# A two-block transformer kernel: latent attention's transposed weights in three rotating PSUM banks and copied by two engines, value products spread over units, one row store moved to a later stage

## The chip, the cores and the metric

The program runs on one core of one Trainium2 chip. Its engines work side by side: TensorE (PE; its weight loads are listed apart as PEld), VectorE (DVE), ScalarE (ACT), GpSimd (POOL), and SyncE (SP), whose queue issues most of the DMAs. The metric is the device time of one execution in microseconds (us), as a median of runs.

## The reference

Two blocks run one after the other on 512 tokens of width 1024. The part that matters here is the beginning of the first block:

```python
sc, scc = silu(c), silu(c_ctx)
shift1, scale1, gate1, ... = split(sc @ w_mod + b_mod)     # only the first two are needed at once
h  = modulate(rms_norm(x, norm1_g), shift1, scale1)        # 512 tokens
hc = modulate(rms_norm(ctx, norm1_g), ...)                 # 256 context tokens
proj = h @ w_in                                            # keys, values, gates, queries, ...
# gated linear attention (GLA): log decays, cumulative sums in chunks of 64 tokens, exponentials of them,
# states per chunk, outputs
# latent attention: 8 query heads, 2 key heads, 512 queries, 512 + 256 keys, head width 128
sc_ = einsum('bkgqd,bknd->bkgqn', q, k) * 128 ** -0.5
p   = softmax(sc_, axis=-1)
y_att = einsum('bkgqn,bknd->bkgqd', p, v)
```

Hyena filters, the merge of three branches, a mixture of 16 experts and the second block follow.

## The kernel before, in words

The program is a row of stages. Each is a block in which every engine has its own list of instructions, written out by hand; semaphores order the engines inside, and at the end of a block all engines meet at a barrier before any of them begins the next. Weights go through a ring of four SBUF slots of 1 MB (`Ring`): SP issues a chunk as soon as the chunk four places ahead of it has been released. A chunk of `w_in` is split by ScalarE into a rounded high part (line 124) and by GpSimd into the low remainder (line 130), and TensorE multiplies high by high, high by low and low by high (lines 240, 243, 244).

The stages that the change and the prediction touch, in order:

- `mod_stage` (0 to 45 us): silu(c) and its products with `w_mod`. SP issues the eight chunks of `w_mod`, then the store of silu(c) from SBUF to the DRAM row `silu_row` (line 350; 128 partitions x 8 single numbers, written element by element), then four loads for the router (line 353), then the first four chunks of `w_in`, and waits until the store and the router loads have landed (`inputs_in`, line 355). `silu_row` is read again only in the merge stage at 685 us (line 456).
- `gla_project_stage` (45 to 175 us) runs `groups_stage` with `gla_decay_work` beside it: functions hung into each engine's list at places (group, place). ScalarE's last ones were the copies of the transposed key tiles for units 2 and 3 (`copy(act, 2)`, line 1162) and the exponential of the chunk totals `K.tot` (line 1169), both behind the four silu evictions of the last group (line 1032).
- `gla_chunk_stage` (175 to 221 us): the chunk states (TensorE lines 1358 and 1367, VectorE's recurrences at line 1456).
- `qk_stage` (221 to 317 us): queries and keys. GpSimd loads `k_cos`, `k_sin` and `k_swap` first; TensorE needs `k_swap` at line 735.
- `latent_attention_stage` (317 to 453 us), written in `attention_stage`: 8 heads of 4 blocks of 128 queries, 32 units in all. It is the only stage that calls this function.

A unit `a` of the attention goes through these steps: TensorE's scores (line 1520, 512 + 256 columns in two PSUM banks, alternating between banks 0-1 and 2-3), VectorE's maximum (line 1563) and bias (1569), ScalarE's exponential with its row sum (1546), VectorE's reciprocal (1574) and scaling (1576), TensorE's six 128 x 128 transposes (1528) into PSUM banks 4 and 5, VectorE's copy of all 768 columns to SBUF `PT` (1584). The loops are skewed: in round `a` TensorE does the scores of unit a and the transposes of unit a - 2. After the last unit of a head it does the head's six value products of 512 columns in one piece (called at line 1536, recorded as line 263), and ScalarE copies the result out (1553). The waits that order this for TensorE:

```python
pe.wait_ge(exp_done, a - 1)      # scores a reuse the banks of unit a-2
pe.wait_ge(normed, b + 1)        # b = a - 2, the block to be transposed
pe.wait_ge(copied, b)            # banks 4, 5 emptied by VectorE's copy of unit b-1
```

A product of fp32 operands is recorded as two MATMUL rows, a transpose as one.

## Time and profile before

| | |
|---|---|
| median of 3 runs | 2266.17 us (2265.34 to 2267.31) |
| the profiled execution's own time | 2269.96 us |
| its span (first to last instruction) | 2268.2 us |
| TensorE busy, share of the span | 2080.7 us, 92% |
| VectorE, ScalarE, GpSimd | 1173.8 (52%), 853.9 (38%), 577.8 us (25%) |
| mean granted TensorE clock | 0.963 |
| stage of latent attention | 317.5 to 452.8 us |

A busy TensorE is not the same as a TensorE at its peak: a matmul's record begins when it is issued and its end is modelled, so records overlap. What a group of them costs is read from start to start.

### The profile page before, as it was taken

What the parts mean: (1) busy time and instruction counts of PE and PEld (TensorE: products, weight loads), DVE (VectorE), ACT (ScalarE), POOL (GpSimd) and SP (SyncE); (2) the same over time, 40 slices, a digit from 0 to 9 for tenths busy, and PEclk for the clock granted to TensorE, in tenths of its full rate; (3) what the DMA queues carried; (4) which work ended last, traced back from release to release, by engine and by line L of the source; (5) the groups of instructions that cost most, each with busy time, mean ns of one, the idle gap of its engine ahead of it and who ended that gap; (6) DMA issues with size and microseconds to landing.
All of it is one profiled execution on the core that took longest, in us unless ns stands there. A gap on an engine that the chain in (4) does not pass through costs nothing. (4 is left out here: it accounts for less than half of the span.)

```text
span 2268.2 us, 23240 instructions
## 1 busy us (share of the span) xinstructions
PE 2080.7 (92%) x9310; PEld 1584.0 (70%) x9310; DVE 1173.8 (52%) x1391; ACT 853.9 (38%) x1059; POOL 577.8 (25%) x191
## 2 busy tenths in 40 slices
PE   5998998899879999889999989999799998999997
PEld 2666754474348888577777767687688876878886
DVE  2444556545884576468888667305703246223223
ACT  3532223234222223357777547514422323212221
POOL 0322200130014344120000023440144444433441
PEclk8999999999989999989999999999999999999999
DMA  7224210031015555279999942231022332322310
GB/s 246 93 74 163 75 37 1 0 112 33 0 37 195 167 195 181 89 285 367 381 382 385 334 163 93 79 106 34 21 92 88 100 119 94 110 93 74 100 48 38
DMA packets 172014, 299.67 MB, mean 132 GB/s; under 512 B 10211, under 2 KB 67754, under 8 KB 171912
## 3 DMA queue, kind: packets, MB, share of 16 engines
q1 hardware_dynamic: 166600, 279.93, 35.8%
q0 software_dynamic: 3008, 9.93, 1.2%
q10 hardware_dynamic: 2304, 8.39, 0.9%
q8 instruction: 71, 1.16, 0.2%
q14 instruction: 31, 0.25, 0.0%
HBM read 275.09 MB, written 23.13 MB: 131 GB/s over the span
## 5 line engine op out<-in xcount | busy, mean ns | idle before, releaser
L130 POOL TENSOR_TENSOR region<-weights,region 128x2048 fp32r<-128x2048 f32 (+2 forms) x94 | 370.8, 3946 | 986.4 <-ACT region L124 736.4
L240 PE MATMUL ps<-region 128*128 128x512 f32 (+1 forms) x1336 | 529.0, 396 | 43.7 <-DVE region L576 12.8
L243 PE MATMUL ps<-region 128*128 128x512 f32 (+1 forms) x1336 | 519.2, 389 | 0.0
L244 PE MATMUL ps<-region 128*128 128x512 f32 (+1 forms) x1336 | 519.2, 389 | 0.0
L240 PEld LDWEIGHTS ps<-region 128*128 128x128 f32 x1336 | 258.8, 194 | 106.9 <-DVE region L130 20.8
L243 PEld LDWEIGHTS ps<-region 128*128 128x128 f32 x1336 | 258.6, 194 | 51.7 <-issue 3.6
L244 PEld LDWEIGHTS ps<-region 128*128 128x128 f32 x1336 | 258.4, 193 | 50.2
L124 ACT ACTIVATE region<-weights 128x2048 fp32r<-128x2048 f32 (+2 forms) x98 | 158.7, 1622 | 291.2 <-PE ps L244 244.6
L2982 DVE TENSOR_TENSOR region<-weights,region 128x2048 fp32r<-128x2048 f32 x92 | 209.4, 2288 | 47.0 <-ACT region L2891 46.8
L2891 ACT ACTIVATE region<-weights 128x2048 fp32r<-128x2048 f32 x92 | 176.2, 1918 | 68.2 <-DMA weights<-moe_w_up 29.8
L281 PE MATMUL ps<-region 128*128 128x512 f32 x480 | 190.0, 396 | 7.2 <-DVE region L4085 4.5
L3928 POOL TENSOR_TENSOR region<-weights,region 128x2048 fp32r<-128x2048 f32 x30 | 143.0, 4781 | 203.8 <-ACT region L4038 178.3
L283 PE MATMUL ps<-region 128*128 128x512 f32 x480 | 187.0, 390 | 0.0
L282 PE MATMUL ps<-region 128*128 128x512 f32 x480 | 186.8, 389 | 0.0
L2780 PE MATMUL ps<-region 128*128 128x512 f32 x384 | 154.2, 401 | 12.6 <-issue 8.0
L2781 PE MATMUL ps<-region 128*128 128x512 f32 x384 | 151.2, 394 | 0.0
L2782 PE MATMUL ps<-region 128*128 128x512 f32 x384 | 151.2, 394 | 0.0
L2404 DVE TENSOR_TENSOR region<-ps,region 128x512 f32<-128x512 f32 x48 | 33.1, 690 | 198.1 <-PE ps L244 198.1
L281 PEld LDWEIGHTS ps<-region 128*128 128x128 f32 x480 | 90.2, 188 | 29.2 <-DVE region L4089 6.0
L4093 DVE TENSOR_TENSOR region<-ps,region 128x512 f32<-128x512 f32 x64 | 44.3, 692 | 124.2 <-PE ps L283 124.2
L4038 ACT ACTIVATE region<-weights 128x2048 fp32r<-128x2048 f32 x32 | 60.3, 1910 | 122.1 <-PE ps L4015 118.2
L283 PEld LDWEIGHTS ps<-region 128*128 128x128 f32 x480 | 90.1, 188 | 19.0
(442 smaller groups left out, 2740.5 us busy)
## 6 DMA issues: line engine op xcount, KB each, us to landing
weights<-w_in SPq DMA_DIRECT2D x54, 1024.0 KB, 5.3
weights<-moe_w_gate SPq DMA_DIRECT2D x32, 1024.0 KB, 7.8
weights<-moe_w_up SPq DMA_DIRECT2D x32, 1024.0 KB, 8.8
weights<-moe_w_down SPq DMA_DIRECT2D x32, 1024.0 KB, 7.7
region<-w_mod_rows SPq DMA_DIRECT2D x32, 512.0 KB, 4.6
weights<-w_mlp_in SPq DMA_DIRECT2D x16, 1024.0 KB, 5.2
weights<-w_mlp_out SPq DMA_DIRECT2D x16, 1024.0 KB, 5.0
weights<-w_mod SPq DMA_DIRECT2D x8, 1024.0 KB, 9.4
```

Of the source, the lines that this page charges most:

```text
L124: act.activation(flat(self.part(K, n, 0)), flat(r.view(n)), ACT.Copy).then_inc(self.hi_done, 1)
L130: eng.tensor_tensor(flat(self.part(K, n, 1)), flat(self.ring.view(n)), flat(self.part(K, n, 0)).bitcast(F32), ALU.subtract).then_inc(self. ...
L240: ins = pe.matmul(out, l_hi, r_hi, start=(start and k == 0), stop=False)
L243: pe.matmul(out, l_hi, r_lo, start=False, stop=False)
L244: ins = pe.matmul(out, l_lo, r_hi, start=False, stop=(stop and k == kt - 1))
L281: pe.matmul(out, w_hi, x_hi, start=(n == 0), stop=False)
L282: pe.matmul(out, w_hi, x_lo, start=False, stop=False)
L283: last = pe.matmul(out, w_lo, x_hi, start=False, stop=(n == len(triples) - 1))
L2780: pe.matmul(K.ps[:, bank, :], x_hi[:, x, :], w_hi[:, k, :], start=(start and k == 0), stop=False)
L2781: pe.matmul(K.ps[:, bank, :], x_hi[:, x, :], w_lo[:, k, :], start=False, stop=False)
L2891: act.activation(flat(part(c, 0)), r.slots[n % RING][:, :], ACT.Copy).then_inc(hi_done, 1)
L2982: dve.tensor_tensor(flat(part(c, 1)), r.slots[n % RING][:, :], flat(part(c, 0)).bitcast(F32), ALU.subtract).then_inc(r.used, 1)
```

## The change

There are three edits.

1. Latent attention. The transposes of a unit go as four (128 x 512) into one bank and two (128 x 256) into another, out of banks 4, 5 and 7 in rotation. VectorE copies the four, ScalarE the two. TensorE waits for ScalarE's copy of unit b - 2 ahead of the first four, and for VectorE's copy of unit b - 1 ahead of the other two. The six value products of head h are put behind the transposes of the next four units, 1, 2, 1 and 2 of them.
2. The store of silu(c) is taken out of `mod_stage` and issued as SP's first DMA in `qk_stage`, which waits for it at its end.
3. In `gla_decay_work` the exponential of the totals moves to ScalarE's place (3, 1), right behind the other exponentials, and the copies for units 2 and 3 to place (4, 0), ahead of the last group's evictions.

```diff
@@ -346,13 +346,10 @@
             sp.dma_start(K.xT, T["xT"].rearrange("(t p) n -> p t n", p=P)).then_inc(x_in, 16)
             sp.dma_start(K.hcT, T["ctxT"].rearrange("(t p) n -> p t n", p=P)).then_inc(ctx_in, 16)
             r.issue_until(sp, n0 + 2 * GROUPS)
-            sp.wait_ge(act_ready, 1)
-            sp.dma_start(K.silu_row.rearrange("o (t p) -> p (o t)", p=P), sc[:, :, 0],
-                         allow_slow_non_contiguous=True).then_inc(inputs_in, 16)
             for dst, src in router_loads(K):
                 sp.dma_start(dst, src).then_inc(inputs_in, 16)
             r.issue_until(sp, n0 + 2 * GROUPS + RING)
-            sp.wait_ge(inputs_in, 80)
+            sp.wait_ge(inputs_in, 64)
 
         @block.scalar
         def _(act):
@@ -628,7 +625,7 @@
     r, T = K.ring, K.T
     split = K.split1
     (raw_done, sq_done, ss_done, mean_done, rec_done, rstd_done, gained, swap_done, t1_done, t2_done, added, out_done,
-     v_done, v_copied, ctx_done, zero_done, select_done, rows_done, cols_done, scale_rec, *out_signals) = K.signals(28 + 1)
+     v_done, v_copied, ctx_done, zero_done, select_done, rows_done, cols_done, scale_rec, row_out, *out_signals) = K.signals(29 + 1)
     gla, last = GlaOutput(K, out_signals), ST - 1
     sq, t, t1, t2, rec = K.at(100, 2, S), K.at(104, 3, S), K.at(110, 2, S), K.at(114, 2, S), K.at(118, 2, S)
     cos, sin, swap = K.at(124, S), K.at(126, S), K.at(128, P)
@@ -671,7 +668,10 @@
         @block.sync
         def _(sp):
             K.start(sp)
+            sp.dma_start(K.silu_row.rearrange("o (t p) -> p (o t)", p=P), K.sc[:, :, 0],
+                         allow_slow_non_contiguous=True).then_inc(row_out, 16)
             r.issue_until(sp, n0 + 6 + RING)
+            sp.wait_ge(row_out, 16)
 
         @block.tensor
         def _(pe):
@@ -1162,11 +1162,13 @@
             act.activation(K.kend[:, :, u, :], z_of(u).rearrange("p (t c) -> p t c", c=P), ACT.Copy)\
                 .then_inc(copied, 1)
 
+    def exps_and_totals(act):
+        exps(act, 2)
+        act.activation(K.tot[:, :, :], K.tot[:, :, :], ACT.Exp, scale=1 / 16).then_inc(copied, 1)
+
     def last(act):
-        copy(act, 2)
         for c in chains:
             act.wait_ge(c, 2 * STEPS)
-        act.activation(K.tot[:, :, :], K.tot[:, :, :], ACT.Exp, scale=1 / 16).then_inc(copied, 1)
         act.wait_ge(copied, 5)
 
     def step(dve, u, j, f):
@@ -1228,7 +1230,7 @@
     return {"loads": 3, "pool": pool,
             "pe": {(1, 0): lambda pe: decays(pe, 0), (3, 0): turn_and_decays, (4, 0): lambda pe: turn(pe, 2)},
             "act": {(1, 0): lambda act: logs(act, 0), (2, 0): lambda act: exps(act, 0), (3, 0): copy_and_logs,
-                    (3, 1): lambda act: exps(act, 2), (4, 2): last},
+                    (3, 1): exps_and_totals, (4, 0): lambda act: copy(act, 2), (4, 2): last},
             "dve": {(1, 0): both(sums, 0), (2, 1): both(scale, 0), (3, 0): both(sums, 2), (3, 2): both(scale, 2)}}
 
 
@@ -1487,7 +1489,7 @@
 
 
 
-    s_done, max_done, bias_done, exp_done, rec_done, normed, turned, copied, o_done, o_copied = K.signals(10)
+    s_done, max_done, bias_done, exp_done, rec_done, normed, turned, copied, rest_copied, o_done, o_copied = K.signals(11)
     NB, NJ = heads * ST, nk // P
     Pb = K.at(tmp, 3, nk)
     PT = K.at(tmp + 3 * nk / 256, 2, NJ, S)
@@ -1507,12 +1509,23 @@
         def sbank(a):
             return K.ps[:, 2 * (a % 2):2 * (a % 2) + 2, :].rearrange("p b n -> p (b n)")[:, 0:nk]
 
-        def tbank():
-            return K.ps[:, 4:6, :].rearrange("p b n -> p (b n)")[:, 0:nk].rearrange("p (j q) -> p j q", q=P)
+        def turned_at(b):
+
+            low, high = ((4, 5, 7)[(2 * b + i) % 3] for i in range(2))
+            return (K.ps[:, low, :].rearrange("p (j q) -> p j q", q=P),
+                    K.ps[:, high, 0:nk - 512].rearrange("p (j q) -> p j q", q=P))
+
+        def value_steps(a):
+
+            h, part = divmod(a - 2 - ST, ST)
+            if not 0 <= h < heads:
+                return h, ()
+            cuts = [i * NJ // ST for i in range(ST + 1)]
+            return h, range(cuts[part], cuts[part + 1])
 
         @block.tensor
         def _(pe):
-            for a in range(NB + 3):
+            for a in range(NB + 2 + ST):
                 if a < NB:
                     if a >= 2:
                         pe.wait_ge(exp_done, a - 1)
@@ -1522,33 +1535,48 @@
                 b = a - 2
                 if 0 <= b < NB:
                     pe.wait_ge(normed, b + 1)
+                    low, high = turned_at(b)
+                    if b >= 2:
+                        pe.wait_ge(rest_copied, b - 1)
+                    for j in range(4):
+                        ins = pe.transpose(low[:, j, :], Pb[:, b % 3, j * P:(j + 1) * P], K.ident[:, :])
+                    ins.then_inc(turned, 1)
                     if b >= 1:
                         pe.wait_ge(copied, b)
-                    for j in range(NJ):
-                        ins = pe.transpose(tbank()[:, j, :], Pb[:, b % 3, j * P:(j + 1) * P], K.ident[:, :])
+                    for j in range(4, NJ):
+                        ins = pe.transpose(high[:, j - 4, :], Pb[:, b % 3, j * P:(j + 1) * P], K.ident[:, :])
                     ins.then_inc(turned, 1)
-                b = a - 3
-                if b >= 0 and b % ST == ST - 1:
-                    h = b // ST
-                    pe.wait_ge(copied, b + 1)
-                    if h >= 1:
-                        pe.wait_ge(o_copied, h)
-                    accumulate(pe, K.ps[:, 6, :], [(values(h, j), PT[:, h % 2, j, :]) for j in range(NJ)])\
-                        .then_inc(o_done, 1)
+                h, part = value_steps(a)
+                for j in part:
+                    if j == 0:
+                        pe.wait_ge(copied, ST * (h + 1))
+                        pe.wait_ge(rest_copied, ST * (h + 1))
+                        if h >= 1:
+                            pe.wait_ge(o_copied, h)
+                    ins = pe.matmul(K.ps[:, 6, :], values(h, j), PT[:, h % 2, j, :], start=(j == 0), stop=(j == NJ - 1))
+                    if j == NJ - 1:
+                        ins.then_inc(o_done, 1)
 
         @block.scalar
         def _(act):
-            for a in range(NB + 3):
+            for a in range(NB + 2 + ST):
                 if a < NB:
                     act.wait_ge(bias_done, a + 1)
                     if a >= 3:
-                        act.wait_ge(turned, a - 2)
+                        act.wait_ge(turned, 2 * (a - 2))
                     act.activation(Pb[:, a % 3, :], sbank(a), ACT.Exp, bias=st[:, 1, a:a + 1],
                                    scale=scale if scales is None else scales[:, a:a + 1],
                                    accum_out=st[:, 2, a:a + 1]).then_inc(exp_done, 1)
-                b = a - 3
-                if b >= 0 and b % ST == ST - 1:
+                b = a - 2
+                if 0 <= b < NB:
                     h = b // ST
+                    dest_of = PT[:, h % 2, :, (b % ST) * P:(b % ST + 1) * P]
+                    act.wait_ge(turned, 2 * b + 2)
+                    if h >= 2:
+                        act.wait_ge(o_done, h - 1)
+                    act.activation(dest_of[:, 4:NJ, :], turned_at(b)[1], ACT.Copy).then_inc(rest_copied, 1)
+                h, part = value_steps(a)
+                if NJ - 1 in part:
                     act.wait_ge(o_done, h + 1)
                     act.activation(dest(h), K.ps[:, 6, :], ACT.Copy).then_inc(o_copied, 1)
                 if first and a in (NB - 3, NB - 1):
@@ -1577,11 +1605,12 @@
                         .then_inc(normed, 1)
                 b = a - 2
                 if b >= 0:
-                    dve.wait_ge(turned, b + 1)
                     h = b // ST
+                    dest_of = PT[:, h % 2, :, (b % ST) * P:(b % ST + 1) * P]
+                    dve.wait_ge(turned, 2 * b + 1)
                     if h >= 2:
                         dve.wait_ge(o_done, h - 1)
-                    dve.tensor_copy(PT[:, h % 2, :, (b % ST) * P:(b % ST + 1) * P], tbank()).then_inc(copied, 1)
+                    dve.tensor_copy(dest_of[:, 0:4, :], turned_at(b)[0]).then_inc(copied, 1)
 
 
 def latent_attention_stage(K):
```

On TensorE, in the attention stage, the head boundary stood like this before (line 1520: scores, 1528: transposes, 263: value products):

```order
L1528 MATMUL ps<-ident,region 128x128 x6
L263 MATMUL ps<-region 128x512 x6
L1520 MATMUL ps<-region 128x512
L1520 MATMUL ps<-region 128x256
L1528 MATMUL ps<-ident,region 128x128 x6
L1520 MATMUL ps<-region 128x512
L1520 MATMUL ps<-region 128x256
L1528 MATMUL ps<-ident,region 128x128 x6
```

The same stage now (1533: scores, 1542 and 1547: the four and the two transposes, 1556: value products):

```order
L1533 MATMUL ps<-region 128x512
L1533 MATMUL ps<-region 128x256
L1542 MATMUL ps<-ident,region 128x128 x4
L1547 MATMUL ps<-ident,region 128x128 x2
L1556 MATMUL ps<-region 128x512
L1533 MATMUL ps<-region 128x512
L1533 MATMUL ps<-region 128x256
L1542 MATMUL ps<-ident,region 128x128 x4
L1547 MATMUL ps<-ident,region 128x128 x2
L1556 MATMUL ps<-region 128x512 x2
```

The value products have moved from one piece of six to one or two behind each unit's transposes; their number is the same.

On ScalarE, the end of `gla_project_stage` was (1139: exponentials, 124: high part of a chunk, 1032: evictions with silu, 1162: key copies, 1169: totals):

```order
L1139 ACTIVATE region<-region 128x512 x2
L1139 ACTIVATE region<-region 128x768
L124 ACTIVATE region<-weights 128x2048
L1032 ACT_TABLE_LOAD
L1032 ACTIVATE region<-ps 128x512 x4
L1162 ACTIVATE region<-ps 128x6x128 x2
L1169 ACT_TABLE_LOAD
L1169 ACTIVATE chunk_decay<-chunk_decay 128x36
```

and is now (1167: totals; the copies keep line 1162):

```order
L1139 ACTIVATE region<-region 128x512 x2
L1139 ACTIVATE region<-region 128x768
L1167 ACTIVATE chunk_decay<-chunk_decay 128x36
L124 ACTIVATE region<-weights 128x2048
L1162 ACTIVATE region<-ps 128x6x128 x2
L1032 ACT_TABLE_LOAD
L1032 ACTIVATE region<-ps 128x512 x4
```

The evictions are the last thing that ScalarE does in this stage, and one table load is gone.

On SP, in `mod_stage`, the queue behind the last chunks of `w_mod` was

```order
L350 DMA silu_row<-silu_c 128x8x1
L353 DMA router<-router_w 128x8x16
L353 DMA router<-router_b 128x16
L353 DMA router<-k_upto 128x128
L353 DMA router<-k_slot_no 128x128
L87 DMA weights<-w_in 128x4x128 x2
```

and is now

```order
L350 DMA router<-router_w 128x8x16
L350 DMA router<-router_b 128x16
L350 DMA router<-k_upto 128x128
L350 DMA router<-k_slot_no 128x128
L87 DMA weights<-w_in 128x4x128 x2
```

Everything behind the store moves up by one place.

## Rows read from the trace of the kernel before

**Rows 1.** Timeline, one head of latent attention: start us, duration, engine, line, operation.

```profile
351.87 5.32 PE L263 MATMUL ps<-region 128*128 128x512 f32 x12
...
357.02 1.45 PE L1520 MATMUL ps<-region 128*128 128x512 f32 x4
...
358.31 0.82 PE L1528 MATMUL ps<-ident,region 128*128 128x128 f32 x6
358.51 0.96 DVE L1563 TENSOR_REDUCE region<-ps 128x1 f32<-128x768 f32 x1 [4.82 <-PE ps L1520]
...
358.96 1.46 PE L1520 MATMUL ps<-region 128*128 128x512 f32 x4
...
360.30 0.95 DVE L1584 COPY region<-ps 128x768 f32<-128x768 f32 x1
...
361.40 0.84 PE L1528 MATMUL ps<-ident,region 128*128 128x128 f32 x6 [0.98 <-DVE region L1584]
...
362.95 0.95 DVE L1584 COPY region<-ps 128x768 f32<-128x768 f32 x1
```

**Rows 2.** Groups by line and form: busy us, mean ns of one, idle before.

```profile
L1546 ACT ACTIVATE region<-ps,region 128x768 f32<-128x768 f32 x32 | 31.7, 990 | 51.2 <-DVE region L1569 51.2
L1033 DVE COPY region<-ps 128x512 f32<-128x512 f32 x10 | 6.9, 690 | 63.5 <-PE ps L244 60.9 <-PE ps L263 2.5
L781 ACT ACTIVATE region<-ps 128x256 f32<-128x256 f32 x6 | 2.2, 371 | 3.2 <-PE ps L244 3.2
```

**Rows 3.** Timeline, the last two groups of value products of the stage.

```profile
429.46 5.32 PE L263 MATMUL ps<-region 128*128 128x512 f32 x12
...
443.63 8.50 PE L263 MATMUL ps<-region 128*128 128x512 f32 x12 [1.05 <-DVE region L1584]
```

**Rows 4.** Stretches: length, busy (x) of PE, PEld, DVE, ACT, POOL, clock, DMA share, GB/s.

```profile
357.00:400.00 43.00, 36.97 (x149) 21.02 (x148) 31.02 (x60) 14.76 (x27) 0.00 (x0) 1.00 0.00 1
...
440.00:442.00 2.00, 0.93 (x5) 0.96 (x6) 0.93 (x1) 0.17 (x1) 1.75 (x1) 0.50 0.00 0
```

**Rows 5.** Timeline of SP and VectorE, end of the mod stage and start of the next.

```profile
27.15 0.51 SPq L350 DMA_DIRECT2D silu_row<-silu_c  x1
...
38.20 0.16 DVE L429 SCALAR_TENSOR_TENSOR gains<-mods,vec_cols 128x8 f32<-128x8 f32 x1
38.21 0.43 SPq L353 DMA_DIRECT2D router<-k_slot_no  x1
...
45.18 1.41 DVE L567 SCALAR_TENSOR_TENSOR region<-region,gains 128x512 f32<-128x512 f32 x2 [6.83 <-remote]
```

**Rows 6.** Line 350: us from issue to landing of the store of silu(c).

```profile
DMA to landing us min/median/max: 13.9/13.9/13.9
```

**Rows 7.** A stretch ahead of the store's landing, columns as in rows 4.

```profile
34.00:41.00 7.00, 3.79 (x33) 2.26 (x32) 2.25 (x5) 0.70 (x2) 0.00 (x0) 0.95 0.01 1
```

**Rows 8.** Timeline, end of the GLA projection stage and start of the chunk stage.

```profile
171.00 0.60 ACT L1032 ACTIVATE region<-ps 128x512 f32<-128x512 f32 x1 [2.12 <-PE ps L244]
...
173.02 1.28 ACT L1169 ACT_TABLE_LOAD   x1
174.31 0.23 ACT L1169 ACTIVATE chunk_decay<-chunk_decay 128x36 f32<-128x36 f32 x1
...
175.02 1.12 PE L1358 MATMUL ps<-region 128*64 128x128 f32 x8 [4.06 <-PEq L948]
...
178.09 0.29 DVE L1452 COPY region<-ps 128x128 f32<-128x128 f32 x1 [1.92 <-PE ps L1367]
```

**Rows 9.** A stretch of the chunk stage, columns as in rows 4.

```profile
176.00:178.00 2.00, 2.00 (x32) 1.60 (x30) 0.18 (x1) 0.97 (x1) 1.72 (x3) 0.50 0.54 160
```

**Rows 10.** The qk stage: GpSimd's last load, its us to landing, and its first reader.

```profile
222.64 0.54 POOL L663 DMA_DIRECT2D region<-k_swap  x1
...
229.41 1.02 PE L735 MATMUL ps<-region 128*128 128x512 f32 x2
...
region<-k_swap POOLq DMA_DIRECT2D x1, 64.0 KB, 2.9
```

## The prediction

> **What bounds the kernel now.** I read the stretches first, then one head on the timeline, then the two stage ends that the other edits touch. TensorE is busy for 92% of the span, so time can only come from places where it stands or runs slowly. In latent attention it stands: in 43 us of steady heads it has 36.97 us of records at full clock, VectorE 31.02, ScalarE 14.76 [rows 4]. One head [rows 1]: the value products start at 351.87, the next scores at 357.02, so six products take 5.15 us, 0.86 each. The scores run to 358.31 (1.29 us), the transposes to 358.96 (0.65 us). The bound alternates. While the value products run VectorE waits (4.82 us ahead of the maximum at 358.51); in the other units TensorE waits (0.98 us ahead of the transposes at 361.40) for line 1584, the copy that empties banks 4 and 5. VectorE's pace there is 2.65 us a unit (copy at 360.30 to copy at 362.95). The period of a head, from value products at 351.87 to those at 429.46 five heads later [rows 1, 3], is 77.59 / 5 = 15.52 us. TensorE's own work in it is 5.15 + 4 x 1.29 + 4 x 0.65 = 12.91 us.
>
> At the end of the mod stage all engines wait for DMAs: VectorE's last instruction starts at 38.20, its next at 45.18 [rows 5], behind the store and the router loads. At the end of the GLA projection ScalarE alone works, from 171.6 to 174.54, and TensorE stands for 4.06 us [rows 8].
>
> **Edit 1, latent attention.** The same products and transposes are issued, and as many scores. VectorE's copy shrinks from 768 to 512 columns: 690 ns [rows 2] against 950 ns, 0.26 less, so its pace becomes 2.65 - 0.26 = 2.39 us a unit. ScalarE, busy for 14.76 of 43 us or 1.33 a unit [rows 4], gets a copy of 256 columns, 0.37 us [rows 2]: 1.70. TensorE with spread products has 1.29 + 0.65 = 1.94 plus 0.86 or 1.72, so 2.80 or 3.66 us, on average 3.23. It is the longest of the three in every unit, if nothing it waits for is late. I walked one short unit, starting at TensorE's scores of a. The maximum of a starts 1.49 after them (357.02 to 358.51 in rows 1); the bias is ready some 1.06 later, at 2.55; maximum, bias, reciprocal and scaling of a - 1 take 1.79 (358.51 to 360.30), and the shorter copy what is left of the pace, 2.39 - 1.79 = 0.60: VectorE is through at 3.9. TensorE begins the next round at 2.80, has finished its scores at 4.09, and only then needs the scaled block of a - 1, ready at about 3.4, and 0.43 later, at 4.5, the emptied bank, ready at 3.9. ScalarE's exponential of a (0.99 [rows 2], a hand-over ahead and the reading of its sum behind) ends at about 3.9; TensorE needs it for the scores of a + 2, at 6.46. ScalarE's own copy is then done by 4.3 and needed more than a unit later. So no wait is left in a head, and the closest margin is 0.6 us.
>
> Sum of this edit:
> - Six full heads, 15.52 to 12.91: 6 x 2.61 = 15.7.
> - The lead-in, where no value products are interleaved yet and VectorE sets the pace: four copies of 0.26: 1.0.
> - From the start of head 6's products (429.46) to those of head 7 (443.63) there are 14.17 us [rows 3], with only 5.15 + 1.29 + 3 x 0.65 = 8.4 us of work for TensorE. With the products spread, VectorE's chain runs beneath them; what remains is head 7's wait until ScalarE has copied head 6's result out (one bank for the output), 0.25 + 0.60 = about 0.9. Saved: 14.17 - 9.3 = 4.9.
> - The last head's products took 8.50 instead of 5.32 us [rows 1, 3], because TensorE's clock stood at its lower level, 0.50, in a stretch in which it had work for only 0.93 of 2 us [rows 4]. With the chain beneath the products that stretch is gone, so I take the 3.2 us.
>
> Together 24.8. The bounds of this term: no gain beyond TensorE's own work is possible, so 25 is the most. At the other end, each unit could lose the hand-over of a buffer at each of the two waits of its transposes; one hand-over is 0.15 us (the copy of 360.30 ends at 361.25, TensorE starts at 361.40 in rows 1), so 28 x 0.30 = 8.4, and 16 at least.
>
> **Edit 2, the store.** It was issued at 27.15 and landed 13.9 us later, at 41.05 [rows 5, 6]. From 34 to 41 all DMA engines together move 1 GB/s and are busy for 1% [rows 7]. The queue is silent for 7 us with the store at its head; the router loads land only after it and SP can issue the last of them only at 38.21. Without the store the router loads should land by about 36 and the first chunks of `w_in` soon after. Then VectorE's own chain, ending at 38.36, ends the stage. A barrier takes 0.48 (ScalarE's last end at 174.54, TensorE's start at 175.02 [rows 8]), so the next stage starts at 38.84 and not at 45.18: 6.3 earlier. Bounds: the stage can't end before its own arithmetic, so 6.3 is the most; if the 1024 short reads of `router_w` are what is slow, hardly anything is won, 0.5.
>
> In the qk stage the store is SP's first DMA. The next chunk has to wait for TensorE to free a slot, so none stands behind the store. GpSimd's three loads go out at the same time. `k_swap` lands at 222.64 + 2.9 = 225.5 and is first read at 229.41 [rows 10], a cover of 3.9 us. If the store's 7 us delayed it fully, TensorE would wait 3.1. I take 0 and keep 3.1 for the range.
>
> **Edit 3, the GLA end.** Gone from behind the last eviction are two key copies, a table load and an exponential; the end moves from 174.54 to 171.60, 2.9 us [rows 8]. The copies now stand ahead of the evictions, where TensorE's next bank comes every 2.7 us and ScalarE waits 2.12 of it [rows 8]: the copies, 1.4 us between 171.60 and 173.02, hide there. Then a second effect. TensorE's pause falls from 4.06 to about 1.2 us. The chunk stage ran its first products at half clock (0.50 at 176 to 178 [rows 9]), and VectorE, whose chain of recurrences sets that stage's first part, could start only at 178.09, 3.1 us after TensorE. With the clock kept, about half of that, 1.4 us, is saved. Bounds: 0 if the clock falls anyway, 1.6 at most.
>
> The Trainium skill (ScalarE: Activation LUTs, "What ACT_TABLE_LOAD costs") puts a switch of tables at 2.66 us, a drain of 1.38 us included. In this trace the activation starts 1.29 us after the load does [rows 8], so the drain doesn't show; by the page edit 3 would be worth 1.4 us more. I go by the row.
>
> **Sum.** 24.8 + 6.3 + 2.9 + 1.4 = 35.4 us. The profiled execution took 2269.96 us (span 2268.2), 3.8 above the median of the runs; there the sum gives 2234.6. Against the median of 2266.17 it is 2230.8, **2231**. All else only shifts: at both ends of latent attention the DMA queues move nothing [rows 4], so the later stages find the same state.
>
> **The rivals.**
> - The heads don't become bound by TensorE alone: gaps of up to 0.3 us in each unit remain at the two-part transposes. For it speaks the margin of 0.6 us only, against it that scores and transposes already follow each other without a gap after two satisfied waits [rows 1]. Edit 1 is then worth 16: 2239.
> - `router_w` is the slow transfer, not the store. For it: also 1024 descriptors. Against it: the store, ahead in the queue, itself landed only at 41.05 [rows 5, 6]. Edit 2 is worth 0.5: 2237.
> - The store holds up GpSimd's three loads in the qk stage: plus 3.1, 2234. The Trainium skill (DMA: Bandwidth & Descriptors, on issuing engines) has all queues share the same 16 DMA engines, which is this case; no row here shows two queues with a store of this kind.
> - Slower: the rotation makes a unit serial. TensorE's transposes wait for a copy by ScalarE, which stands behind an exponential, which waits for VectorE, which waits for TensorE. The chain of one unit is 3.9 to the end of its exponential as walked above, and about 0.8 for reciprocal and scaling, 0.65 for transposes and 0.9 for a copy and its hand-over: 6.2 us. With two units in flight it costs 3.1 a unit, under 3.23. If only one were in flight, 32 x 6.2 = 198 us against 135, that is 63 us more in edit 1, less the 10.6 of the others: 2319. It decides from 4.2 us a unit (15.52 / 4 = 3.88, plus those 10.6 us over 32 units). The waits as written, on units b - 1 and b - 2, allow two; little speaks for it.
>
> **How the numbers follow.** Forecast as summed 0.62, gaps 0.13, `router_w` 0.11, qk stage 0.10, slower 0.02, the rest for something unseen. 2231 belongs to the first; its own spread is 2227 to 2235. The range has to take in the second and third, so up to 2241; below, the edges of the terms give 2227, and a little of the 3.8 us by which two executions of one kernel differ makes it 2226. A change below 0.2% (4.5 us) could not be told from none here. Faster 0.97, same 0.015, slower 0.015.
>
> **What would show it.** In the changed kernel's trace: TensorE without idle time from the first head to the last, period 12.9 us; VectorE waiting 0.4 to 1.3 us in every unit instead of 4.8 once a head; clock 1.00 to the stage's end, the last products 5.3 us; the next stage after the mod stage at 38.8; the last activation of the GLA projection a silu eviction, and VectorE's first copy in the chunk stage 1.6 us after TensorE's start; `k_swap` read without a wait. The prediction is wrong if VectorE or ScalarE shows up as what releases the transposes in the heads, or if the DMA silence at 34 us stays.

## The result, and the profile after

The changed kernel takes 2252.09 us (median of 4 runs, 2248.19 to 2254.9) beside 2266.74 for the kernel before: ratio 0.9934, 95% interval 0.9916 to 0.9951. That is 14.7 us faster where 35 were forecast, and 11 us above the upper end of the range. A second comparison of the same two kernels gave 0.9895 (0.9874 to 0.9915), 24 us. The two intervals meet end to end (0.9915 and 0.9916) without overlapping, so comparisons scatter by more than one interval tells; both lie short of the forecast's 0.984. A few us are therefore read from the lengths of stages below, and not from whole times.

The first instruction of TensorE (in the GLA projection of VectorE) after each barrier cuts the profiled executions into stages. Lengths in us:

| stage | before | after | difference | forecast |
|---|---|---|---|---|
| mod stage | 45.18 | 39.76 | -5.42 | -6.3 |
| GLA projection | 129.84 | 124.53 | -5.31 | -2.9 |
| chunk stage | 46.12 | 44.82 | -1.30 | -1.4 |
| qk stage | 96.39 | 102.65 | +6.26 | 0 |
| latent attention | 135.70 | 116.62 | -19.08 | -24.8 |
| all that follows | 1814.97 | 1818.02 | +3.05 | 0 |
| span | 2268.2 | 2246.4 | -21.8 | -35.4 |

Three rows are missed by more than 2.5 us: qk, attention and what follows. (The profiled executions lie 21.8 us apart and the medians 14.7: the profile before took longer than any of its four runs, the profile after is that of its fastest.) I take what the forecast had right first. Timeline of latent attention, as rows 1:

```profile
339.58 1.45 PE L1533 MATMUL ps<-region 128*128 128x512 f32 x4
...
340.87 0.60 PE L1542 MATMUL ps<-ident,region 128*128 128x128 f32 x4
341.07 0.96 DVE L1591 TENSOR_REDUCE region<-ps 128x1 f32<-128x768 f32 x1 [1.19 <-PE ps L1533]
...
341.31 0.38 PE L1547 MATMUL ps<-ident,region 128*128 128x128 f32 x2
...
341.53 1.02 PE L1556 MATMUL ps<-region 128*128 128x512 f32 x2
...
343.88 0.96 DVE L1591 TENSOR_REDUCE region<-ps 128x1 f32<-128x768 f32 x1 [0.32 <-PE ps L1533]
...
344.33 1.88 PE L1556 MATMUL ps<-region 128*128 128x512 f32 x4
...
352.52 1.45 PE L1533 MATMUL ps<-region 128*128 128x512 f32 x4
```

No wait stands on TensorE in this head. It takes 352.52 - 339.58 = 12.94 us (forecast 12.91), and VectorE waits 0.32 or 1.19 a unit (forecast 0.4 to 1.3). The two ends of the stages, as rows 5 and 8:

```profile
39.06 0.16 DVE L426 SCALAR_TENSOR_TENSOR gains<-mods,vec_cols 128x8 f32<-128x8 f32 x1
39.76 0.75 DVE L564 SCALAR_TENSOR_TENSOR region<-region,gains 128x512 f32<-128x512 f32 x1 [0.54 <-DVE gains L426]
```

```profile
163.39 0.60 ACT L1032 ACTIVATE region<-ps 128x512 f32<-128x512 f32 x1 [2.12 <-PE ps L244]
...
164.29 0.66 PE L1360 MATMUL ps<-region 128*64 128x128 f32 x8 [0.94 <-PEq L948]
...
166.02 0.29 DVE L1454 COPY region<-ps 128x128 f32<-128x128 f32 x1 [0.57 <-PE ps L1369]
```

The mod stage ends by VectorE's arithmetic, with a wait of 0.54 us where 6.83 stood, and from 34 to 41 us the DMA queues move 253 GB/s where they moved 1 [rows 7]. A silu eviction is ScalarE's last instruction in the GLA projection, TensorE pauses for 0.94 us instead of 4.06 [rows 8], and VectorE's first copy comes 1.73 us behind TensorE (forecast 1.6).

Now the losses. The qk stage, timeline of SP, GpSimd and TensorE, as rows 10:

```profile
209.21 0.40 SPq L671 DMA_DIRECT2D silu_row<-silu_c  x1
...
210.61 0.54 POOL L660 DMA_DIRECT2D region<-k_swap  x1
...
222.13 1.35 PE L735 MATMUL ps<-region 128*128 128x512 f32 x2 [4.58 <-DMA region<-k_swap]
```

and the DMAs of 190 to 300 us (KB of one, median us from issue to landing):

```profile
DMA packets 4406, 6.97 MB, mean 63 GB/s; under 512 B 1184, under 2 KB 1184, under 8 KB 4400
...
region<-k_cos POOLq DMA_DIRECT2D x1, 256.0 KB, 11.7
...
region<-k_swap POOLq DMA_DIRECT2D x1, 64.0 KB, 11.4
silu_row<-silu_c SPq DMA_DIRECT2D x1, 4.0 KB, 9.3
```

`k_swap` took 11.4 us instead of 2.9 [rows 10], behind a store of 4 KB. TensorE waited 4.58 us for it, and its clock then was 0.64 from 222 to 225 us. Together the stage lost 6.3.

In latent attention one place is off, in the first unit after the last head's scores have begun to run out:

```profile
407.01 4.50 POOL L130 TENSOR_TENSOR region<-weights,region 128x2048 fp32r<-128x2048 f32 x1 [124.05 <-ACT region L124]
407.03 4.90 DVE L1604 TENSOR_SCALAR region<-region 128x768 f32<-128x768 f32 x1
...
411.99 1.11 PE L1542 MATMUL ps<-ident,region 128*128 128x128 f32 x4 [3.45 <-DVE region L1604]
...
413.32 3.62 PE L1556 MATMUL ps<-region 128*128 128x512 f32 x4
...
416.85 4.53 POOL L130 TENSOR_TENSOR region<-weights,region 128x2048 fp32r<-128x2048 f32 x1 [5.34 <-ACT region L124]
...
417.70 0.69 DVE L1613 COPY region<-ps 128x512 f32<-128x512 f32 x1 [2.06 <-PE ps L1542]
```

VectorE's scaling, 0.62 us everywhere else, took 4.90. GpSimd's subtraction (the low part of the next stage's first weight chunk) had begun 0.02 us earlier, and the scaling ended 0.42 after it. TensorE stood for 3.45 us and did its next products at half clock (from 413 to 416 us the granted clock is 0.50: 1.2 GHz and not 2.4). The row at 417.70 narrows it: VectorE's copy out of PSUM ran at its usual 0.69 us beneath the second subtraction. What the subtraction stops is the scaling, which reads and writes SBUF; in all seven profiled executions with edit 1 and the subtraction in this place, this one and those below, one scaling takes 4.90 or 4.91. The Trainium skill says this (SBUF — State Buffer, "Who interferes with whom"): VectorE and GpSimd share a pair of SBUF ports, whoever issues first holds it for the whole instruction, the other blocks, and a scalar multiplication can be of the kind that needs it. This trace agrees, with 4.90 against 0.62 us. In the kernel before, the same two instructions met in the other order:

```profile
429.80 0.62 DVE L1576 TENSOR_SCALAR region<-region 128x768 f32<-128x768 f32 x1
430.04 4.76 POOL L130 TENSOR_TENSOR region<-weights,region 128x2048 fp32r<-128x2048 f32 x1 [141.31 <-ACT region L124]
```

There the scaling came first and kept its 0.62 us, and it was the subtraction that took longer, 4.76 instead of 4.50 us.

### The profile page after: what moved, and what is told of

The parts are those of the page before. It is cut to its first block and busy times, and to the rows that moved or that the text cites. A ratio compares the mean times of both kernels' runs of the same rounds, so it can differ in the third digit from the quotient of the medians.

```text
span 2246.4 us, 23296 instructions
## 1 busy us (share of the span) xinstructions
PE 2074.2 (92%) x9310; PEld 1584.6 (71%) x9310; DVE 1172.9 (52%) x1391; ACT 861.1 (38%) x1090; POOL 578.7 (26%) x191
```

## The experiments

The theory after these readings: the three edits do what the forecast said, and two collisions, one that it had missed and one that it had put at nothing, take back 6 us each (store against `k_swap`, subtraction against scaling). The rival: the rest is lost downstream, because later stages meet the DMA queues in another state.

**The changed kernel again, and each edit alone** (the hunks of the diff above for attention, for the store, or for `gla_decay_work`, on the kernel before).

> The changed kernel once more, for its ratio and for a second profile. Theory 1 (the missing gain was lost in two places ahead of 430 us: TensorE's wait for k_swap with its clock behind it, about 6 us, and a 3.45 us stall of TensorE at 408 us with its clock behind it, about 6 us): the profile shows both again, and the stretch from the start of the Hyena projection to the end takes what it took before, 1815 us, within 3. Theory 2 (the kernel also grows behind the attention, by the 4 to 7 us by which most executions are longer than the profiled one): that stretch takes 1819 to 1823 us.

> The kernel before with edit 1 alone. Theory 1: 19 us less in the attention stage (24.8 of the forecast less the stall and the slow clock), nothing elsewhere: 2247 to 2249, ratio 0.992. The scaling instruction on VectorE beside GpSimd's subtraction lasts some 5 us instead of 0.62. Theory 2: several us given back behind the stage, ratio 0.994 to 0.996.

> The kernel before with edit 2 alone: the store of silu(c) leaves the mod stage and goes to the head of SP's queue in the qk stage. Theory 1: the mod stage ends 6.3 us earlier, the qk stage is 6.2 us longer, so the kernel is within 1 us of before. Rival (the store costs nothing in the qk stage and the wait for k_swap is a scatter of that one execution): 6 us faster, ratio 0.9973, and k_swap is read without a wait.

> The kernel before with edit 3 alone. By the sum of the prediction 2.9 us from the stage's end and 1.4 from TensorE's clock in the chunk stage: 4.3 us faster, ratio 0.998. Rival (the clock falls anyway): 2.9 us, ratio 0.9987, and granted clock 0.5 in the first 5 us of the chunk stage.

Measured side by side, with 2268.88 us for the kernel before; lengths of the stages in the profiled execution:

| kernel | us | ratio (95%) | mod | GLA | chunk | qk | attention | rest |
|---|---|---|---|---|---|---|---|---|
| changed, again | 2244.97 | 0.9895 (0.9874 to 0.9915) | 38.70 | 123.36 | 44.76 | 102.94 | 114.15 | 1816.8 |
| attention only | 2248.56 | 0.9911 (0.9889 to 0.9934) | 45.56 | 126.70 | 45.32 | 96.40 | 116.28 | 1817.6 |
| store only | 2267.30 | 0.9988 (0.9972 to 1.0004) | 39.15 | 126.51 | 44.09 | 103.61 | 134.11 | 1817.5 |
| GLA end only | 2264.41 | 0.9976 (0.9963 to 0.9990) | 47.30 | 126.72 | 44.92 | 96.40 | 134.17 | 1814.0 |

The qk stage is 6 to 7 us longer exactly where the store is in it, and attention is 18 to 22 us shorter exactly where edit 1 is. The store alone gives nothing that the whole times can tell from zero (the ratio's interval reaches from 6 us faster to 1 us slower); the stages tell it: what the mod stage gives (6 us) the qk stage takes. The rest of the program takes 1814.0 to 1817.6 us here and 1811.4 to 1820.1 in the kernels below. Both ends of that range have edit 1 and the store moved. The mean of the three profiles without edit 1 is 1815.5, that of the eleven with it 1816.9. So the rival as a loss of several us falls; the 3.05 us of the table above lie inside the scatter, and a loss of 1 or 2 us can't be excluded.

The GLA projection scatters too, from 123 to 130 us, and here the granted clock sorts it. In the stretches from 12 to 36 and from 66 to 84 us behind the stage's start some executions have clocks of 0.93 and 0.72, others of 0.93 and 0.91. With the first pair the stage takes 129.84 us without edit 3 (the kernel before) and 126.72 with it (GLA end only); with the second pair 126.51 without (store only) and 123.36 with it (changed, again). So at equal clock edit 3 shortens the stage by 3.1 to 3.2 us. In the first profile only this part of the 5.31 us belongs to the edit; the rest is the clock, and why it differs from one execution to the next is open. In the GLA end kernel TensorE's clock is 1.00 in the first 32 us of the chunk stage, so the rival of that run (the clock falls anyway) falls.

**The store elsewhere.** In the latent attention stage, or in its stage behind GpSimd's loads:

```diff
 # store in attention: taken out of qk_stage's SP block, put into attention_stage's
+            sp.dma_start(K.silu_row.rearrange("o (t p) -> p (o t)", p=P), K.sc[:, :, 0],
+                         allow_slow_non_contiguous=True).then_inc(row_out, 16)
+            sp.wait_ge(row_out, 16)
 ...
 # store behind the loads: in qk_stage, ahead of the store
+            sp.wait_ge(K.loaded, K.loads(3))
```

> The changed kernel with the store of silu(c) issued by SP in the latent attention stage instead of the qk stage. Theory 1 (in the qk stage the store keeps the landing of k_swap back, and TensorE's first swap product waits 4.58 us for it and then runs behind at half clock): k_swap lands about 3 us after its issue again, the qk stage is back from 102.7 to 96.4 us, the kernel 6 us faster than the changed one, about 2246 against 2252 (beside the kernel before a ratio near 0.990 if the changed one has 0.9925). No other engine waits for SP in the attention stage before its end, so the store costs nothing there. Rival (the three loads by GpSimd are slow for a reason of their own, such as what the stage before left in the queues): the qk stage stays at 102.7 and k_swap's landing near 11 us.

> The changed kernel, where SP in the qk stage waits until GpSimd's three loads have landed and only then issues the store. If it is the order of store and loads that costs the wait: k_swap lands in about 3 us, the qk stage takes 96.4 us, 6 us less than in the changed kernel. If instead the store costs the stage something by itself wherever it lies in it (SP stands behind it before it can ask for the next weights), the stage stays above 100 us, with TensorE waiting for a weight chunk later in it.

Measured: 2244.35 us (ratio 0.9855, 0.9830 to 0.9880) and 2241.22 us (0.9859, 0.9834 to 0.9884), beside 2272.44. The changed kernel wasn't measured beside them, and its two medians, 2252.09 and 2244.97, differ by more than the 6 us in question, so the stages decide. The qk stage took 96.43 and 96.40 us, `k_swap` landed in 3.0 us in both, while the store itself needed 9.4 and 8.6. So the store costs the stage nothing where nobody's load is behind it. Theory 1 holds and both rivals fall: it is the order of store and loads in the first few us of the stage.

**GpSimd's subtractions behind the last scaling.**

```diff
         def _(pool):
+            pool.wait_ge(normed, NB)
             for n in first:
                 split.low(K, pool, n)
```

> The changed kernel, where GpSimd in latent attention waits for the last scaling before its first subtraction. Theory 1 (GpSimd's subtraction at 407.01 keeps VectorE's scaling from ending, 4.90 us instead of 0.62, and TensorE loses 3.45 us of wait and the full clock behind it): all 32 scalings take 0.62 us (mean about 620 ns instead of 754), TensorE has no wait above 1 us before the last products, and the stage takes 110 to 111 us instead of 116.6; the kernel is 6 us faster than the changed one, about 2246. Rival (TensorE would have run out of work there anyway, since VectorE's chain is the tighter one behind a fourth unit): the stage stays within 2 us of 116.6. Rival 2: the subtractions, now later, hold up the next stage, whose products read the low halves: TensorE waits there for up to 10 us at its start.

> The changed kernel with both changes: the store in latent attention, and GpSimd's subtractions there behind the last scaling. If the two losses are all that separates the forecast from the result: 12 us faster than the changed kernel, about 2234 to 2240, ratio to the kernel before near 0.985, stages qk 96.4 and latent attention 110 to 111 us. If one loss hid another (a later wait for weights, the clock), less than 9 us.

With the wait alone: 2239.03 us, ratio 0.9843 (0.9820 to 0.9867). Groups by line and form (count, busy us, mean ns), first of the changed kernel, then of this one:

```profile
L1604 DVE TENSOR_SCALAR region<-region 128x768 f32<-128x768 f32 x32 | 24.1, 754 | 1.1
```

```profile
L1605 DVE TENSOR_SCALAR region<-region 128x768 f32<-128x768 f32 x32 | 19.9, 620 | 1.1
```

The 134 ns of the mean are one instruction's 4.28 us spread over 32: such a loss hides well in a mean. Latent attention took 110.31 us, 6.3 less than 116.62, and the next stage started as before (its wait at the start 1.10 us in both). Both rivals fall. The whole kernel gained more than the 6 us expected over the changed one (0.9843 beside 0.9895); the stages account for 4 to 6 of it, as follows.

The 6.3 us are the price in the first profile, where the clock fell behind the wait. The changed kernel, again, met the same collision and the same wait:

```profile
409.98 0.66 PE L1542 MATMUL ps<-ident,region 128*128 128x128 f32 x4 [3.45 <-DVE region L1604]
```

There the granted clock stayed at 1.00 (from 409 to 418 us), the products behind it ran at full speed, and the stage took 114.15 us, 3.9 more than 110.21 and not the 6 that were expected of this loss. The kernel with neighbouring DRAM addresses, below, kept its clock behind this wait as well; in the other four such executions it fell to 0.50 to 0.69 for some us. So the collision costs 3.9 us by itself and up to 2.5 more where the clock falls. Why it falls in one execution and not in another stays open.

With the store in attention as well: 2233.99 us (2231.01 to 2235.77), ratio 0.9832 (0.9813 to 0.9851). Its stages: qk 96.40, attention 110.21. Timeline of GpSimd, then of TensorE, end of attention:

```profile
407.59 9.00 POOL L130 TENSOR_TENSOR region<-weights,region 128x2048 fp32r<-128x2048 f32 x2 [128.80 <-DVE region L1605]
```

```profile
411.31 5.39 PE L1557 MATMUL ps<-region 128*128 128x512 f32 x12 [0.78 <-ACT region L1582]
...
417.80 0.47 PE L240 MATMUL ps<-region 128*128 128x512 f32 x1 [1.10 <-PEq L1494]
```

This kernel has the lowest median of all, though its interval overlaps that of the wait alone: 38 us less than before by its ratio, where the forecast had 35.4. Some of that is luck of the execution: its two mended stages explain 10.5 to 12.7 us over the changed kernel's two profiles, and in its profile the rest of the program took 1811.4 us, the shortest of all.

**What makes a 4 KB store hold the queues for 9 us?** First, neighbouring addresses on the DRAM side; then a source whose eight numbers lie side by side as well. Neither kernel leaves the right row behind (the first permutes it, the second stores other numbers), so they serve to time the qk stage and are no versions to use.

```diff
-            sp.dma_start(K.silu_row.rearrange("o (t p) -> p (o t)", p=P), K.sc[:, :, 0],
+            sp.dma_start(K.silu_row.rearrange("o (p t) -> p (o t)", p=P), K.sc[:, :, 0],
 # second kernel
+            sp.dma_start(K.silu_row.rearrange("o (p t) -> p (o t)", p=P), K.sc[:, 0, 0:8]).then_inc(row_out, 16)
```

> The changed kernel, with the store of silu(c) in its place in the qk stage, but written in runs of 8 neighbouring values for each partition: 128 pieces of 32 bytes and not 1024 of 4. The row then holds silu(c) in another order, so what the later stages read from it is permuted. If the number of small pieces is what keeps the queues busy: k_swap lands in about 3 us, no wait of TensorE for it, and the qk stage takes 96.4 us as against 102.7. If it is any store ahead of the loads that delays them: the landing stays near 11 us and the stage at 102.7.

> The changed kernel with another source for the store in the qk stage: eight neighbouring numbers of each partition (the first column's padded block, so the row of silu(c) holds other numbers), written in 128 pieces of 32 bytes. In the run with the 32 byte runs on the DRAM side alone, the source was still strided by 128 bytes and the queues still counted about 1184 packets under 512 bytes in the stage, so it did not test the number of pieces. Here that count should fall by 896 to about 290. If the number of single pieces is what holds the queues: store and k_swap land in about 3 us, TensorE has no wait for k_swap, the qk stage takes 96.4 us. If any store there delays the loads: k_swap lands after 8 us or more and the stage stays above 98 us.

The first gave 2242.24 us (0.9890, 0.9859 to 0.9920), beside 2269.24. Its expectation was worked from a wrong premise: the pieces were not 32 bytes, since the queues still counted 1186 packets under 512 bytes. The store took 9.4 us again, `k_swap` 8.5, TensorE waited 1.7 us and the stage took 98.22. The second gave 2238.71 us (0.9871, 0.9839 to 0.9903), beside 2268.70, with these DMAs from 190 to 300 us:

```profile
DMA packets 3510, 6.97 MB, mean 63 GB/s; under 512 B 288, under 2 KB 288, under 8 KB 3504
...
region<-k_swap POOLq DMA_DIRECT2D x1, 64.0 KB, 2.8
silu_row<-silu_c SPq DMA_DIRECT2D x1, 4.0 KB, 1.4
```

896 packets fewer, the same bytes: the store lands in 1.4 us instead of 9.3, `k_swap` is not delayed, the stage is back at 96.40 us. With the bytes equal, it is the cutting into 1024 single pieces that costs, and GpSimd's queue pays for SP's store. The Trainium skill (DMA: Bandwidth & Descriptors, "Rules for kernel authors") says that a last dimension with gaps becomes one descriptor per element; the packet counts of these two traces agree (1184 against 288).

**Which part of edit 1 brings the gain?** Both kernels are the one with both losses mended.

```diff
 # copies on VectorE: ScalarE's copy taken out, and behind VectorE's
+                    dve.wait_ge(turned, 2 * b + 2)
+                    dve.tensor_copy(dest_of[:, 4:NJ, :], turned_at(b)[1]).then_inc(rest_copied, 1)
 # products in one
-            cuts = [i * NJ // ST for i in range(ST + 1)]
-            return h, range(cuts[part], cuts[part + 1])
+            return h, range(NJ) if part == 0 else ()
```

> The kernel with both losses mended, where VectorE copies all six turned blocks in two instructions and ScalarE none. By the walk behind the forecast TensorE's own work, 3.23 us a unit, is the longest: VectorE's pace would be 2.39 plus some 0.4 for the second copy, 2.8 us a unit. Then steady heads stay at 12.9 us and only the lead-in and the short units lose a little: latent attention 110.2 plus 1 to 3 us. If ScalarE's share of the copies were what brought the gain, the head goes back towards 14 us or more and the stage to 118 or more.

> The kernel with both losses mended, where the six value products of a head are issued together again and not spread over its units; banks and copies stay as changed. If the spreading is what brought the gain: VectorE waits once a head beneath the block of products (about 4.8 us) and TensorE waits for VectorE or ScalarE in the other units, with a head near 15.52 - 4 x 0.26 = 14.5 us, and the stage at 110.2 + 6 x 1.6 + about 4 at its end, 122 to 126 us. If the three rotating banks alone do it: heads of 12.9 us and a stage below 113.

The kernel before took 2269.24 us beside these two. Copies on VectorE: 2238.99 us (0.9863, 0.9835 to 0.9891), attention 112.07 us, 1.9 over 110.21, in the 1 to 3 expected. Products in one: 2245.30 us (0.9888, 0.9860 to 0.9916), attention 121.45 us, 11.2 over, just below the 122 expected. Its timeline:

```profile
334.90 5.32 PE L1556 MATMUL ps<-region 128*128 128x512 f32 x12
...
341.54 0.96 DVE L1591 TENSOR_REDUCE region<-ps 128x1 f32<-128x768 f32 x1 [4.59 <-PE ps L1533]
...
363.35 5.32 PE L1556 MATMUL ps<-region 128*128 128x512 f32 x12
```

Two heads in 28.45 us, 14.22 each (14.5 expected), and VectorE waits 4.59 us beneath the block again. So of the 24 to 25 us that edit 1 is worth, 11.2 are the spreading; the other 13 to 14 come from the banks and the shorter copies together, with the products still in one block and GpSimd's subtractions moved; no run separates these. ScalarE's share of the copies adds only 1.9 once the products are spread: without it VectorE is busy for 59.1 of the 70 us from 330 to 400 instead of 52.7, and the steady heads still take 12.94 us, so VectorE has time over.

## Why the prediction was wrong

**Edit 1, the steady heads** (6 x 2.61): right. Period 12.94 for 12.91, no wait on TensorE.

**Edit 1, from head 6's products to the end:** the mechanism was right, and the step that failed is the sentence that with the products spread "VectorE's chain runs beneath them". It did, but the walk took every scaling at its usual length (0.62 us, inside its 1.79), and one took 4.90. In the kernel before, GpSimd's first subtraction at 430.04 fell 0.24 us behind the start of a scaling, and the next scaling (437.37) came only after head 6's block of products, when the subtraction was over; the spread products close this gap. The forecast has no term for the two subtractions. Price: 3.45 us of wait, 3.9 in all where the clock held (changed, again), 6.3 where it fell (the first profile). With it mended the stage takes 110.2 to 110.3, a gain of 25.4, where 24.8 were forecast with 25 as the most. The bound was passed only against that one execution. The 3.2 us for the last products were partly that one execution's: 8.50 us there, but 7.35 and 7.51 in the store and GLA kernels, which have the old attention. Against those (134.1 us) edit 1 is worth 24. The sign "clock 1.00 to the stage's end" failed in the changed kernel's first profile (0.50 from 413 to 416 us).

**Edit 2, the mod stage:** right. The stage ends by its arithmetic, 5.4 us earlier in the first profile and 6.0 and 6.5 in two others; the store was the slow transfer and not `router_w`, which falls as a rival.

**Edit 2, the qk stage:** wrong, by "I take 0". The mechanism stood there as a rival at 0.10 with a price of 3.1. Both halves failed. The rows of the store itself (1024 pieces, 13.9 us, silent queues) [rows 6, 7] spoke for a delay, and the 0 rested on no row, only on the loads having another queue. And the price took the store's 7 us of silence as the delay and left out the clock: the measured delay is 8.5 us (11.4 - 2.9), of which 4.58 reach TensorE, and 1.7 more go to the products at a lower clock.

**Edit 3:** the pause fell from 4.06 to 0.94 us as forecast. By itself the edit gave 0.9976, 5.4 us (interval 2 to 8), for 4.3. The first effect is 3.1 us, by the pause and by the stage at equal clock, where 2.9 were forecast. The second effect is smaller than 1.4: VectorE's first copy follows TensorE by 3.07 us in the first profile but by 2.25 and 2.44 in two others without the edit, and by 1.73 with it, so 0.5 to 0.7. The length of the chunk stage doesn't show it: 46.12, 45.32 and 44.09 us without the edit, 44.76 to 44.92 with it. The -1.30 of the first table beside the forecast's -1.4 is luck: the shortest chunk stage of all has no edit 3.

**Sum.** 35.4 less 6.3 less 6.3 is 22.8, beside 21.8 in the profiles and 14.7 and 23.9 in the two comparisons. The 21.8 hides scatter both ways: the GLA projection gave 2.2 more than its edit, the rest of the program took 3.05. For the second execution the same sum is 35.4 less 6.5 less 3.9, 25.0, beside 23.9 measured. Why the first comparison shows the least of all stays open. The serial unit, the rival on the other side, didn't appear.

## What to carry to other kernels

When a stage is packed tighter, list every instruction of the engines that are not on its path, GpSimd's above all, and ask for each what it could stop when it falls elsewhere; a collision that cost nothing beneath a gap can cost most of its length (3.45 us of wait from a scaling 4.28 us too long), and sometimes the clock behind it, when the gap is gone. Price a store by its pieces as well as by its bytes, and expect loads issued behind it, on another queue too, to pay: put a store of single elements where no load follows, or make its elements neighbours. Where a rival has rows for it and the chosen value has none, the rival is the forecast.

## What the runs showed of the hardware

- A store of 4 KB in 1024 pieces of 4 bytes lands after 8.6 to 9.5 us in the qk and attention stages (13.9 in the mod stage), in 128 pieces after 1.4; loads of 64 to 256 KB that GpSimd issues up to 1.4 us behind the first kind land after 11.4 to 11.9 us instead of 2.6 to 3.0. With neighbouring DRAM addresses but a strided source the store is as slow (9.4), yet the loads behind it land after 6.8 (`k_cos`) to 8.5 us (`k_swap`).
- A scaling from SBUF to SBUF of 128x768 that VectorE starts 0.02 us behind GpSimd's subtraction takes 4.90 us instead of 0.62; the other way round, a subtraction that starts 0.24 us behind the scaling takes 4.76 instead of 4.50. A copy of 128x512 from PSUM beneath such a subtraction keeps its 0.69 us.
- A pause of TensorE and its clock: behind a pause of 3.45 us the granted clock fell (0.50 from 413 to 416 us) in the changed kernel's first profile and stayed at 1.00 in its second. Behind pauses of 4.58 to 4.83 us for `k_swap` it was 0.50 to 0.62 in the next 3 us in four executions. Behind one of 4.06 us ahead of the chunk stage it was 0.50 from 2 to 4 us later in three kernels; behind one of 0.94 us it stayed at 1.00.
